# The last norm of a hybrid decoder step: second-choice expert rows loaded plainly and added by GpSimd, and four products moved ahead of TensorE's last wait

## What is computed

```
x = layer_norm(ALPHA * x + hier_moe(x), ln3_g, ln3_b)
hier_moe: every token has two chosen experts (a first and a second choice);
          y(token) = gate1 * expert_a(token) + gate2 * expert_b(token)
```

## Time and profile before

| what | value |
|---|---|
| median of 3 runs | 676.91 us (676.42 to 678.39) |
| profiled execution, its own time | 678.53 us |
| its span, first to last instruction | 676.8 us |
| mean granted TensorE clock | 0.989 |
| PE busy | 645.1 us, 95% |
| PEld busy | 395.5 us, 58% |
| DVE busy | 323.7 us, 48% |
| ACT busy | 156.6 us, 23% |
| POOL busy | 208.6 us, 31% |
| bytes moved by DMA | 146.14 MB |

### The profile page before, as it was taken

One profiled execution on the slowest core, in us unless ns is written; L12 is line 12 of the kernel. 1 busy time (PEld: TensorE's weight loads), 2 busy tenths in 40 slices (PEclk: granted clock), 3 DMA queues, 4 the chain that ended last, 5 costly groups with the idle time before them and its releaser, 6 DMA issues.

```text
span 676.8 us, 8651 instructions
## 1 busy us (share of the span) xinstructions
PE 645.1 (95%) x3276; PEld 395.5 (58%) x3276; DVE 323.7 (48%) x756; ACT 156.6 (23%) x345; POOL 208.6 (31%) x245
## 2 busy tenths in 40 slices
PE   6999899999999999999999999999999999999982
PEld 3445588887788764446896784444574454333330
DVE  0283447227555973745000875355872424244445
ACT  1113401102542220002111740222324111121144
POOL 4240001002567555513000885012244332111231
PEclk9999999999999999999999999999989999999997
DMA  8994405303363154067940787454449999999598
GB/s 296 390 316 162 140 1 186 125 1 127 96 209 115 62 206 140 16 183 225 384 179 16 240 307 288 185 213 186 181 160 362 413 412 403 376 347 411 205 203 170
DMA packets 45811, 146.14 MB, mean 216 GB/s; under 512 B 5738, under 2 KB 6058, under 8 KB 41663
## 3 DMA queue, kind: packets, MB, share of 16 engines
q1 hardware_dynamic: 31559, 107.50, 42.5%
q0 software_dynamic: 12032, 33.29, 17.3%
q10 hardware_dynamic: 2176, 4.76, 1.8%
HBM read 130.34 MB, written 20.33 MB: 223 GB/s over the span
## 4 chain that ended last, share of the span: by engine, by line
PE 87%; DMA 5%; DVE 3%; ACT 2%; issue 1%; POOL 0%; DVEq 0%; ACTq 0%; POOLq 0%
PE ps L463 17%; PE ps L740 13%; PE ps L1073 12%; PE ps L497 8%; PE ps L576 7%; PE ps L1093 5%; PE ps L578 4%; DMA xn<-y_d 3%; PE ps L836 2%; PE ps L765 2%; PE ps L960 2%; PE ps L649 2%; PE ps L1054 1%; PE ps L664 1%; PE ps L820 1%; PE ps L525 1%
## 5 line engine op out<-in xcount | busy, mean ns | idle before, releaser
L463 PE MATMUL ps<-xT,wring 128*128 128x208 f32 (+1 forms) x512 | 113.7, 383 | 0.3 <-ACT xT L1351 0.3
L463 PEld LDWEIGHTS ps<-xT,wring 128*128 128x128 f32 x512 | 93.2, 190 | 19.0 <-issue 0.4
L740 PE MATMUL ps<-wring,P 128*128 128x512 f32 x224 | 99.2, 596 | 0.0
L740 PEld LDWEIGHTS ps<-wring,P 128*128 128x128 f32 x224 | 41.6, 190 | 49.1 <-issue 49.0
L1073 PE MATMUL ps<-wring,P 128*32 128x512 f32 (+1 forms) x288 | 65.3, 600 | 0.9 <-DVE P L2304 0.9
L497 PE MATMUL ps<-wring,P 128*128 128x512 f32 x128 | 57.5, 607 | 1.0 <-DVE P L1714 0.8
L2465 POOL TENSOR_SCALAR rstd<-agg 128x1 f32<-128x1 f32 (+1 forms) x15 | 16.8, 1121 | 112.1 <-DVE agg L1699 112.0
L2304 DVE COPY P<-ps 128x512 f32<-128x512 f32 x11 | 7.6, 692 | 76.4 <-PE ps L1054 71.0
L1073 PEld LDWEIGHTS ps<-wring,P 128*32 128x32 f32 (+1 forms) x288 | 22.2, 130 | 36.2 <-issue 36.2
L497 PEld LDWEIGHTS ps<-wring,P 128*128 128x128 f32 x128 | 24.5, 195 | 30.7 <-issue 30.5
L2607 POOL TENSOR_TENSOR P<-P,xT 128x2048 f32<-128x2048 f32 x8 | 36.0, 4528 | 20.9 <-DMA xT<-sq_d 19.0
(11 more groups left out here) (444 smaller groups left out, 1090.0 us busy)
## 6 DMA issues: line engine op xcount, KB each, us to landing
wring<-in_w_in SPq DMA_DIRECT2D x5, 2048.0 KB, 8.6
wring<-in_w_gate SPq DMA_DIRECT2D x10, 1024.0 KB
wring<-in_w_up SPq DMA_DIRECT2D x10, 1024.0 KB
P<-in_w_down SPq DMA_DIRECT2D x10, 1024.0 KB, 11.1
P<-in_cache_mem_k SPq DMA_DIRECT2D x8, 1024.0 KB, 6.7
P<-in_cache_mem_v SPq DMA_DIRECT2D x8, 1024.0 KB, 5.4
y_d<-P POOLq DMA_DIRECT2D x1, 4160.0 KB, 27.4
wring<-in_ca_wv SPq DMA_DIRECT2D x2, 2048.0 KB, 20.8
```

Of the source, the lines that this page charges most:

```text
L463: last = mm(out, lhs(k), rhs(k), start=(k == 0), stop=(k == n - 1))
L740: last = mm(bk[:, :], src[:, k, START[t]:START[t] + TR], w[:, k, :], start=(k == 0), stop=(k == KC - 1))
```

## The change

It has two parts.

**GpSimd and SP.** Only the five first-choice transfers and the samples' second-choice transfer stay accumulating DMAs. The first choices go first, in the order of `LAST_NORM`: (0,S) (0,0) (0,1) (0,2) (0,4); then, after (0,S) has landed, (1,S). The second choices of the prompt's tiles are loaded by SP with three plain DMAs (tile 0, tile 1, tiles 2 and 4 together; 0.5, 0.5 and 1 MB) into gate and up slot 1, after waits for that slot's last user and for all scatters. GpSimd adds each to `xn` with a 128x1024 `tensor_tensor`, after waits for the first choice's landing and the load, and counts `choice_added`. VectorE waits for that too; on a prompt tile `x3_in` now ends at 16.

**TensorE.** Ahead of the wait for the last pass stand now the samples' products of the first kept pass and four of the first kept pass's products (tiles 0 and 1, both halves). Behind it: the samples' products of the second kept pass, `sum_full` 1, and the rest.

The diff (the waits in the branch for an overflow, which isn't taken, are left out):

```diff
+        CHOICE_SLOT = 1
+        loads_of = lambda t: 32 if t == SAMPLES else 16
+        second_choice = gu_slots[CHOICE_SLOT].rearrange("p (t d) -> p t d", t=NQT)
...
@@ TensorE @@
             tiles = LAST_NORM[1:]
+            add_samples(0, ps[6])
+            for j in range(2):
+                for q in range(2):
+                    add_kept(0, ps[2 * j + q], tiles[j], q, start=True, stop=False)
             pe.wait_ge(y_act, NPASS)
             pe.wait_ge(y_dve, NPASS)
-            for i in range(KEPT):
-                last = add_samples(i, ps[6])
-            last.then_inc(sum_full, 1)
+            add_samples(1, ps[6]).then_inc(sum_full, 1)
             for j, t in enumerate(tiles):
                 if j == 3:
                     pe.wait_ge(y_act, NPASS + 1)
                     pe.wait_ge(y_dve, NPASS + 1)
                 for q in range(2):
-                    add_kept(0, ps[2 * j + q], t, q, start=True, stop=False)
+                    if j >= 2:
+                        add_kept(0, ps[2 * j + q], t, q, start=True, stop=False)
                     add_kept(1, ps[2 * j + q], t, q, start=False, stop=True).then_inc(sum_full, 1)
@@ SP, after the weight loads @@
+            sp.wait_ge(gu_full, 1 + RELEASE[max(n for n in range(NE) if n % WS == CHOICE_SLOT)])
+            for i in range(3):
+                sp.wait_ge(y_out[i], 16 * SCATTERS[i])
+            for j in range(2):
+                sp.dma_start(second_choice[:, j, :], y_choice[1, TR * j:TR * j + TR, :]).then_inc(choice_in[j], 16)
+            sp.dma_start(second_choice[:, 2:4, :], y_choice[1, 2 * TR:4 * TR, :].rearrange("(t p) d -> p t d", p=TR)).then_inc(choice_in[2], 16)
@@ VectorE, per tile @@
-                dve.wait_ge(x3_in[t], 32)
+                dve.wait_ge(x3_in[t], loads_of(t))
+                if t != SAMPLES:
+                    dve.wait_ge(choice_added, PROMPT.index(t) + 1)
@@ GpSimd @@
-            add_choices(NT, 0)
+            pool.wait_ge(xa_ready, NT)
+            for i in range(3):
+                pool.wait_ge(y_out[i], 16 * SCATTERS[i])
+            for t in LAST_NORM:
+                n = rows_of(t)
+                pool.dma_start(xn[0:n, t, :], y_choice[0, START[t]:START[t] + n, :], accum_op=ALU.add).then_inc(x3_in[t], 16)
+            pool.wait_ge(x3_in[SAMPLES], 16)
+            pool.dma_start(xn[0:NS, SAMPLES, :], y_choice[1, NP_:NTOK, :], accum_op=ALU.add).then_inc(x3_in[SAMPLES], 16)
+            for j, t in enumerate(PROMPT):
+                pool.wait_ge(x3_in[t], 16)
+                pool.wait_ge(choice_in[min(j, 2)], 16)
+                G.tensor_tensor(xn[:, t, :], xn[:, t, :], second_choice[:, j, :], ALU.add).then_inc(choice_added, 1)
```

More of the change, by code:

```diff
@@ L349, in layer_kernel @@
         x3_in = [sem(f"x3_in{t}") for t in range(NT)]
+        choice_in, choice_added = [sem(f"choice_in{j}") for j in range(3)], sem("choice_added")
         xa_ready, tok_ready = sem("xa_ready"), sem("tok_ready")
@@ L1282, in _ @@
                 for t in range(NT):
-                    sp.wait_ge(x3_in[t], 32)
+                    sp.wait_ge(x3_in[t], loads_of(t))
+                sp.wait_ge(choice_added, NQT)
                 for t in range(NT):
@@ L2414, in _ @@
                     x, r = xn[0:n, t, :], rstd[0:n, t:t + 1]
-                    dve.wait_ge(x3_in[t], 64)
+                    dve.wait_ge(x3_in[t], 32 + loads_of(t))
                     V.tensor_reduce(part3[0:n, t, 0:1], x, AX, ALU.add).then_inc(row_parts, 1)
@@ L2674, in _, with add_choices_again @@
                     scatter(p - 5)
-            def add_choices(ready, landed):
-                pool.wait_ge(xa_ready, ready)
+            def add_choices_again():
+                pool.wait_ge(xa_ready, 2 * NT)
                 for i in range(3):
@@ L2682, in add_choices @@
                     if c:
-                        pool.wait_ge(x3_in[t], landed + 16)
+                        pool.wait_ge(x3_in[t], loads_of(t) + 16)
                     pool.dma_start(xn[0:n, t, :], y_choice[c, START[t]:START[t] + n, :], accum_op=ALU.add).then_inc(x3_in[t], 16)
@@ L2698, in _ @@
                 for t in range(NT):
-                    pool.wait_ge(x3_in[t], 32)
+                    pool.wait_ge(x3_in[t], loads_of(t))
+                pool.wait_ge(choice_added, NQT)
                 def step(i, done):
@@ L2717, in _ @@
                     step(2, ov_go)
-                add_choices(2 * NT, 32)
+                add_choices_again()
 _OUTS = [(1, 512, 1024), (8, 1, 1024), (1, 1, 15, 512), (1, 1, 4, 128, 128), (1, 1, 4, 128), (1, 1, 4),
```

## The result

| | before | changed |
|---|---|---|
| median | 677.01 us (6 runs, 676.42 to 678.39) | 683.65 us (6 runs, 681.94 to 684.27) |
| ratio to before | | 1.0096, 95% interval 1.0084 to 1.0108 |
| profiled execution: time, span | 678.53, 676.8 | 684.04, 682.3 |

The changed kernel is 6.6 us slower. The forecast was 4.6 us slower, 681.5 in a range of 677.5 to 684.0.

The account below looks back on a forecast made before the run. It took the end to move with tile 4's start on VectorE, set by the samples' second choice in q0: +4.7 us, less 0.1 for the last stores, so 676.91 + 4.6 = 681.5 us, in a range of 677.5 to 684.0.

Parts of the forecast that it names:

- The chain moves to the samples' start: VectorE's tail: tile 4 starts 11.45 us after the samples or later, and the end moves as much as that start.
- (1,S) behind four tiles: Queue q0: the samples' second choice, issued near 643.8, lands at 658.7, so VectorE starts the samples at 658.75, not 651.40.
- The loads' price: DMA engines: SP's plain loads delay (1,S) by 5.0 us less 1.15 of free time, 3.85 us.
- The products: TensorE's end: the moved products put the samples' sum 2.50 us later, at 652.64, though TensorE ends 1.0 us earlier.
- GpSimd's adds "cost nothing": GpSimd's four adds, 2.26 us each, lie beside the transfers, end at 659.9 and cost nothing.
- Rival C: GpSimd's adds and VectorE slow each other when both run: at most 2.26 us on top, 683.8; chance 0.07.
- a tile stretched beyond 2.9 us: VectorE's tiles: forecast every 2.85 us without a wait; stretching beyond 2.9 us would show the prediction wrong.
- A: DMA engines: the plain loads hide in gaps, (1,S) lands at 654.85; +0.85 us, 677.8; chance 0.12.
- B: Queue q0: (1,S) doesn't queue behind the tiles, TensorE's sum sets the samples' start; -0.15 us, 676.8; chance 0.06.
- D: Kernel's end: B's case, and the last stores land in 1.8 us, not 3.7; -2.05 us, 674.9; chance 0.04.

Follow-up runs that it names:

- fourth experiment: The changed kernel with TensorE's end as before, no product ahead of its last wait: 684.76 us, ratio 1.0104.
- products alone: The kernel before with only the change's TensorE part: 678.68 us, ratio 1.0000.
- third version: Against the changed kernel: plain loads for tiles 0 and 1 only, added before their first-choice transfers; TensorE moves only first-pass samples' products; 674.72 us, ratio 0.9951.

## Why the prediction was right, and where its size was off

**The chain moves to the samples' start: right.** Tile 4's start moved by 6.41 us and the end by 6.2, both from the last scatter on, and every tile followed in 2.85 us. What is behind tile 4's start became 0.2 us shorter, where the forecast had taken 0.1.

**(1,S) behind four tiles: right, and so was its size.** VectorE's samples start 7.18 us later than before; the forecast had 7.35 (658.75 for 651.40). Two parts of it were measured apart: without the loads 3.65 (forecast 3.85), and with the old place in the queue 4.65, where TensorE's sum then holds the start. The long landing, 12.6 us, was put at 15: the issue came 12.55 us after the last scatter's and not 10.4, since it waits for (0,S), which now takes 6.4 us behind the plain loads. The landing itself was where it was forecast, 25.15 for 25.3.

The loads' price is near its forecast partly by luck. Its working was 5.0 us of all engines less 1.15 of free time. In the changed kernel q1's shares from 639 to 652 us add up to some 6.3 us of all engines for these 2.1 MB. Their first data came 6.3 us after the last scatter's issue, where 7.1 had been reckoned, so that more free time lay ahead of (1,S) as well. The two misses offset each other.

**The products: right.** 2.50 us was the working; 2.57 (fourth experiment) and 2.56 (products alone) were measured, and 2.63 for the four tile products without the samples' ones. That the late transfer covers them in the changed kernel was shown.

**GpSimd's adds "cost nothing": this step failed.** The adds were on time for every tile, at 2.34 us each for the 2.26 reckoned. But their cost lies in the operations of VectorE beside them, and the last add still ran when the samples began. Rival C said just that and allowed up to 2.26 us; it was given 0.07 and left out of the sum. Its term measures 1.93 us, and with it the 4.7 us by which tile 4 was to move become 6.6; 6.41 was measured. By one of its own signs, a tile stretched beyond 2.9 us, the prediction was wrong here: from the samples' start to tile 0's it took 4.80. The time stayed inside the range, 0.35 us under its upper end, and that end held half of C.

The forecast's own schedule had the two overlapping by 1.15 us (658.75 to 659.9), and that should have decided. It was 2.07, because the order makes it so: the last add starts when tile 4's first choice lands (657.52 in this trace), and (1,S), next in the queue and small, landed 0.32 us later.

The price could have been read before. The prediction says that no run showed the size, since it looked at rows 3 alone. The trace of before has GpSimd adding and multiplying from 231 to 236 us beside VectorE's adds of two SBUF tensors (L427, nine of them in all). They take 0.69 us alone and up to 1.65 beside GpSimd, and here too the one shown ends 0.55 us after the operation of GpSimd (L2517) that was under way:

```profile
L427 DVE TENSOR_TENSOR P<-P x9: 686/855/1648, 227.0 to 241.3; 128x512 f32<-128x512 f32 x9
```
```profile
231.39 1.42 POOL L2517 TENSOR_TENSOR P<-P,wcb 128x512 f32<-128x512 f32 x1 [4.94 <-DVE cq L1925]
231.95 1.41 DVE L427 TENSOR_TENSOR P<-P 128x512 f32<-128x512 f32 x1
```

The Trainium skill, GPSIMD Engine Reference, Key points, says that GpSimd shares its SBUF interfaces with VectorE and contends with its instructions with two SBUF inputs. The traces here agree, and give it a size.

**The other rivals.** A falls by the run without loads, B by the 12.6 us, D by the result. The Trainium skill's fit of 2.0 us plus bytes at 436 GB/s (DMA: Bandwidth & Descriptors, on the anatomy of a GpSimd DMA) would have given an estimated 2.1 us for 32 KB. The case shows 2.9 with nothing ahead in the queue, and 8.1 and 12.6 by what stood ahead, so here the fit comes near only for the transfer that stands first.

## What to carry to other kernels

When work is moved from a queue to an engine, look at who is first in line behind it: here the smallest transfer, 32 KB that the next engine wants first, was put last in its queue, and that outweighed what the change saved. Moving work ahead of a wait pays only as far as the idle time there reaches: 4.0 us moved into 1.0 us of idle put 2.5 us onto whoever wanted the first result after the wait. And a GpSimd operation on two SBUF tensors has a price on VectorE where that one reads two tensors from SBUF: reckon with the rest of the GpSimd operation that is under way. Put it where VectorE is idle or reads PSUM, as the third version does by adding before the accumulating transfer and not after it.

## What was not expected of the hardware

- Beside adds on GpSimd VectorE's 0.68 us operation with two SBUF inputs took 2.2 to 2.8 us, and a 1.27 us one up to 3.0, while the same instruction with one input in PSUM kept 0.67. It waits out the running add. The adds themselves went from 2.34 to as much as 3.23 us.
- The plain loads didn't take turns evenly with the accumulating transfers: they went nearly first (why isn't shown). The DMA queues of the changed kernel from 640 to 645 us:

```profile
q1 hardware_dynamic: 406, 1.53, 85.1%
q0 software_dynamic: 47, 0.09, 13.3%
```

Tile 0's first choice, issued before 640, released GpSimd's first add only at 650.35, 17.66 us after the last scatter's issue, where it released the next issue at 12.87 before. Here VectorE lost nothing by it, since it waits for (1,S), which stands last anyway. A kernel whose next engine waits for the head of the queue might lose by it; no run shows that.
